# A hybrid decoder block on one core: the first pair's rows picked in turned form, and a new order of the last steps

## The reference, cut to what matters

```python
x = x + hybrid_mixer(rms_norm(x, mix_norm_g), ...)         # mixers, gates, output projection
t = rms_norm(x, ffn_norm_g)                                # 512 tokens
group, expert logits = t @ w_router_group, t @ w_router_expert
# one group of 4 per token, the top 2 of its 8 experts, weights combine (T, 32)
for e in range(32):
    hid = silu(t @ w_expert_gate[e]) * (t @ w_expert_up[e])  # 1024 -> 256
    out += combine[:, e:e+1] * (hid @ w_expert_down[e])      # 256 -> 1024
return rms_norm(x + out, final_norm_g)
```

## Time and profile before

| | us |
|---|---|
| median of 3 runs | 722.11 (720.05 to 722.59) |
| the profiled execution | 720.5 |
| its span, first to last instruction | 718.4 |
| PE busy | 698.4, 97% of the span |
| weight loads (PEld) busy | 514.5, 72% |
| VectorE, ScalarE, GpSimd busy | 371.8, 256.4, 80.1 |
| chain that ended last, share of PE | 90% |
| moved by DMA | 163.52 MB, mean 228 GB/s |

### The profile page before, as it was taken

How to read it: one execution, slowest core, us unless ns; L and a number is a source line. 1 busy time by engine, 2 the same in 40 slices (tenths; PEclk the granted TensorE clock), 3 DMA queues, 4 the chain that set the end, 5 groups by cost and what they waited for, 6 DMA issues and landing times.

```text
span 718.4 us, 10092 instructions
## 1 busy us (share of the span) xinstructions
PE 698.4 (97%) x3967; PEld 514.5 (72%) x3967; DVE 371.8 (52%) x727; ACT 256.4 (36%) x426; POOL 80.1 (11%) x116
## 2 busy tenths in 40 slices
PE   7999999999999999999999999999999999999894
PEld 6888987877877777788888888665555556555442
DVE  6378996357676778755536303751514121212227
ACT  7332134467676776644225212121101111111113
POOL 2001922000010101000003000011211212121000
PEclk9999999999999999999999999999999999999998
DMA  7523244220212222295214598699999999999993
GB/s 240 174 66 111 65 121 147 74 73 16 68 66 73 74 74 74 82 381 181 91 56 183 219 416 303 266 368 365 408 418 419 401 421 421 418 420 417 419 375 141
DMA packets 60208, 163.52 MB, mean 228 GB/s; under 512 B 7846, under 2 KB 39667, under 8 KB 47868
## 3 DMA queue, kind: packets, MB, share of 16 engines
q1 hardware_dynamic: 54668, 150.71, 55.3%
q0 software_dynamic: 5488, 12.11, 4.5%
HBM read 154.64 MB, written 15.99 MB: 238 GB/s over the span
## 4 chain that ended last, share of the span: by engine, by line
PE 90%; DMA 4%; DVE 3%; ACT 1%; issue 1%; SPq 0%; POOLq 0%; DVEq 0%; ACTq 0%
PE psum L1719 31%; PE psum L2146 15%; PE psum L1820 12%; PE psum L2172 8%; PE psum L1999 6%; PE psum L1832 3%; PE psum L2112 2%; DMA ring_e<-y_dram 2%; DVE ring_e L1087 2%; PE psum L1845 1%; PE psum L1875 1%; DMA y_dram<-ye,slots 1%; PE psum L2155 1%; PE psum L1958 1%; PE psum L1910 1%; PE psum L1898 1%
## 5 line engine op out<-in xcount | busy, mean ns | idle before, releaser
L1719 PE MATMUL psum<-xh,wh 128*128 128x512 f32 x256 | 99.9, 390 | 0.8 <-DVE xl L1087 0.8
L1719 PE MATMUL psum<-xh,wl 128*128 128x512 f32 x256 | 99.6, 389 | 0.0
L1719 PE MATMUL psum<-xl,wh 128*128 128x512 f32 x256 | 99.6, 389 | 0.0
L1090 DVE TENSOR_TENSOR wl<-raw,wh 128x1280 fp32r<-128x1280 f32 (+4 forms) x37 | 71.8, 1945 | 24.7 <-ACT wh L780 9.0
L1087 DVE SCALAR_TENSOR_TENSOR hid<-psum,rslot,act_g 128x256 f32<-128x256 f32 x17 | 8.2, 483 | 93.4 <-PE psum L2146 92.8
L1719 PEld LDWEIGHTS psum<-xh,wh 128*128 128x128 f32 x256 | 48.1, 188 | 11.1 <-DVE xl L1087 1.0
L1719 PEld LDWEIGHTS psum<-xh,wl 128*128 128x128 f32 x256 | 48.0, 188 | 9.9
L1719 PEld LDWEIGHTS psum<-xl,wh 128*128 128x128 f32 x256 | 48.1, 188 | 9.8
L1820 PE MATMUL psum<-xh,wh 128*128 128x512 f32 x128 | 51.7, 404 | 0.0
L1820 PE MATMUL psum<-xh,wl 128*128 128x512 f32 x128 | 50.1, 391 | 0.0
L1820 PE MATMUL psum<-xl,wh 128*128 128x512 f32 x128 | 49.9, 390 | 0.0
(11 more groups left out here) (386 smaller groups left out, 1539.6 us busy)
## 6 DMA issues: line engine op xcount, KB each, us to landing
raw<-in_w_gate SPq DMA_DIRECT2D x16, 1024.0 KB, 6.4
raw<-in_w_in SPq DMA_DIRECT2D x9, 1024.0 KB, 5.5
ring_w<-in_w_expert_gate SPq DMA_DIRECT2D x8, 1024.0 KB, 19.8
ring_w<-in_w_expert_up SPq DMA_DIRECT2D x8, 1024.0 KB, 22.4
ring_h<-in_w_expert_down SPq DMA_DIRECT2D x8, 1024.0 KB, 16.5
ring_h<-in_w_expert_gate SPq DMA_DIRECT2D x6, 1024.0 KB, 18.2
ring_e<-in_w_expert_down SPq DMA_DIRECT2D x6, 1024.0 KB, 23.1
ring_e<-in_w_expert_gate SPq DMA_DIRECT2D x6, 1024.0 KB, 21.4
```

What stands on the lines that cost most here:

```text
L1090: return dve.tensor_tensor(dst, src, hi.bitcast(F32), ALU.subtract)
L1719: last = nc.tensor.matmul(dst, a, b, start=start and n == 0, stop=stop and n == len(seq) - 1)
```

## The change

It has three parts. (1) In `choose_rows`, `x2` becomes the stationary operand, 128 features of it at a time (with a step of 8), and `chosen` the moving one. The result comes out turned, in the banks where the transposes would have put it, so the two copies to `xg` and the first turn's transposes go, with the waits for them. (2) In the last turn, `hid` is computed ahead of tile 1's weighted sum. (3) Tile 0's final scaling leaves VectorE: the reciprocal is computed ahead of the adds, ScalarE copies the sum with the scale, and GpSimd multiplies by the gain; SyncE stores tile 0 first, on a semaphore of its own. What else changes are counts at semaphores, and a memset that now covers both halves of `xg`.

```diff
@@ choose_rows (PE)
-                return nc.tensor.matmul(bank[b][:, :], chosen[:, t, :], x2[:, t, b * T:(b + 1) * T], start=t == 0, stop=t == NT - 1)
+                for k in range(4 * b, 4 * b + 4):
+                    last = nc.tensor.matmul(bank[b][:, (k % 4) * P:(k % 4 + 1) * P], x2[:, t, :].rearrange("p (n c) -> p c n", c=KC)[:, k, :],
+                                            chosen[:, t, :], start=t == 0 and k % 4 == 0, stop=t == NT - 1, skip_group_check=True)
+                return last
...
-                choose_rows(NT - 1, b).then_inc(S["routed_ps"], 1)
+                choose_rows(NT - 1, b).then_inc(S["xt_ps"], 1)
@@ x_transposes, expert_pass (PE)
-                if isinstance(c, int) and i == 0:
-                    pe.wait_ge(S["moved_a"], 2 * NT + 1)
-                    pe.wait_ge(S["hot_ready"], ALL_HITS + 1)
-                elif b == 0:
+                if b == 0:
...
-                for b in range(2):
-                    x_transposes(c, 0, first % 2, b)
+                if not isinstance(c, int):
+                    for b in range(2):
+                        x_transposes(c, 0, first % 2, b)
@@ ahead of the expert pass (ScalarE, VectorE, GpSimd)
-            act.wait_ge(S["routed_ps"], NT + 1)
-            act.activation(xg[:, 0, 0:T], bank[0][:, :], ACT.Copy).then_inc(S["moved_a"], 1)
...
-            dve.wait_ge(S["routed_ps"], NT + 2)
-            dve.tensor_copy(xg[:, 0, T:2 * T], bank[1][:, :]).then_inc(S["hot_ready"], 1)
...
-            st.link(pool.memset(xg[:, 1, :], 0.0))
+            st.link(pool.memset(xg[:, :, :], 0.0))
@@ last turn (VectorE)
-                        gather_results(1, EARLY_ROWS)
                     dve.wait_ge(S["silu"], E + 1)
                     dve.wait_ge(S["gu_done"], E + 1)
                     stt(hid[:, :], bank[3][:, 0:FE], rslot[:, column(c, i)], act_g[:, :], ALU.mult, ALU.mult).then_inc(S["hid_r"], 1)
+                    if isinstance(c, int) and i == LAST:
+                        gather_results(1, EARLY_ROWS)
@@ the end (VectorE)
+            dve.wait_ge(S["root"], NT + 2 + NORMED.index(0))
+            dve.reciprocal(stat[:, 2, 0:1], stat[:, 1, 0:1]).then_inc(S["comb"], 1)
             added(2)
-            first_scaled(0)
             added(3)
             first_scaled(2)
@@ the end (ScalarE)
                     final_norm(n, t, TOTALS[t], 3 * NT)
+                    if t == 0:
+                        act.wait_ge(S["comb"], 3)
+                        act.activation(halves(yt[0][:, 1, :]), TOTALS[0], ACT.Copy, scale=stat[:, 2, 0:1]).then_inc(S["norm_step"], 1)
@@ the end (GpSimd)
+            pool.wait_ge(S["tab_in"], 48)
+            pool.wait_ge(S["norm_step"], 2)
+            pool.tensor_tensor(halves(yt[0][:, 1, :]), halves(yt[0][:, 1, :]), halves(gfin), ALU.mult).then_inc(S["norm_step"], 1)
@@ the end (SyncE)
+            sp_e.wait_ge(S["norm_step"], 3)
+            sp_e.dma_start(out_v[0], yt[0][:, 1, :]).then_inc(S["out_done"], 16)
             store_results(0)
```

More of the change, by code:

```diff
@@ L308, in hybrid_trunk @@
             "hi_part xg_ps xg_neg xg_min xg_ln xg_max xg_exp xb_ps xg_free gate_ps br_ps gate_free gate_mul h_add h_hi h_split out_ps x2_ready "
-            "wo_in wo_hi wo_split g_in tab_in x2_out xt2_ps moved_a lg_ps sq2_sum wr_ready slots_in flag_ready lg_act lg_in m_ready routed_ps "
+            "wo_in wo_hi wo_split g_in tab_in x2_out xt2_ps moved_a lg_ps norm_step wr_ready slots_in flag_ready lg_act lg_in m_ready routed_ps "
             "hot_ready slot_ps idx_ready over_ready rs_in rs_ps rs_ready rank_ready turns gf0 gf1 w_ps pick_ready y_hi y_lo y_zero xt_ps xe g_done gu_done silu hid_r "
@@ L606, in store_results @@
                 for n, t in enumerate(NORMED):
-                    sp_e.wait_ge(S["fin_last"], base + n + 1)
+                    if base == 0 and t == 0:
+                        continue
+                    sp_e.wait_ge(S["fin_last"], base + n + (1 if base else 0))
                     sp_e.dma_start(out_v[t], yt[t][:, 1, :]).then_inc(S["out_done"], 16)
+            sp_e.wait_ge(S["norm_step"], 3)
+            sp_e.dma_start(out_v[0], yt[0][:, 1, :]).then_inc(S["out_done"], 16)
             store_results(0)
@@ L623, in _ @@
                 load_results(range(NT))
-                store_results(NT)
+                store_results(NT - 1)
                 sp_e.wait_ge(S["out_done"], 2 * (16 * NT))
@@ L1009, in _ @@
                 token_squares(n)
-            act.wait_ge(S["sq2_sum"], 1)
+            act.wait_ge(S["norm_step"], 1)
             act.activation(stat[:, 1, :], stat[:, 0, :], ACT.Sqrt, bias=eps[:, 0:1], scale=1.0 / D).then_inc(S["root"], 1)
-            act.wait_ge(S["routed_ps"], NT + 1)
-            act.activation(xg[:, 0, 0:T], bank[0][:, :], ACT.Copy).then_inc(S["moved_a"], 1)
             act.wait_ge(S["lg_in"], 1)
@@ L1067, in _ @@
                     final_norm(n, t, TOTALS[t], 3 * NT)
+                    if t == 0:
+                        act.wait_ge(S["comb"], 3)
+                        act.activation(halves(yt[0][:, 1, :]), TOTALS[0], ACT.Copy, scale=stat[:, 2, 0:1]).then_inc(S["norm_step"], 1)
                 else:
-                    act.wait_ge(S["comb"], 2 + t - ADDED + 1)
+                    act.wait_ge(S["comb"], 3 + t - ADDED + 1)
                     final_norm(n, t, halves(yt[t][:, 0, :]), 3 * NT)
@@ L1077, in _ @@
                 for n, t in enumerate(NORMED):
-                    act.wait_ge(S["fin_last"], NT + n)
+                    act.wait_ge(S["fin_last"], NT - 1 + n)
                     final_norm(n, t, TOTALS[t], 4 * NT)
@@ L1422, in _ @@
             dve.wait_ge(S["sq_done"], 3 * NT)
-            dve.reduce_sum(stat[:, 0, :], sq_part[:, :, :], AX.X).then_inc(S["sq2_sum"], 1)
+            dve.reduce_sum(stat[:, 0, :], sq_part[:, :, :], AX.X).then_inc(S["norm_step"], 1)
             for part in range(2):
@@ L1671, in _ @@
             with dve.If(most[0] > SLOT):
-                dve.wait_ge(S["comb"], 2 + NT - ADDED)
+                dve.wait_ge(S["comb"], 3 + NT - ADDED)
                 for t in range(NT):
@@ L2064, in table_products @@
                 if i == SPILL and k == 0:
-                    pe.wait_ge(S["hot_ready"], ALL_HITS + 2)
+                    pe.wait_ge(S["hot_ready"], ALL_HITS + 1)
                     slot_products()
@@ L2188, in _ @@
                 with pe.Fori(1, PASSES) as c:
-                    pe.wait_ge(S["hot_ready"], c + (ALL_HITS + 2))
+                    pe.wait_ge(S["hot_ready"], c + (ALL_HITS + 1))
                     slot_products()
```

## The result

The changed kernel took 728.5 us (median of 4 runs, 727.22 to 731.11), the kernel before beside it 721.3 (4 runs, 720.05 to 722.59): a ratio of 1.0099, with a 95% interval of 1.0065 to 1.0133. The forecast of 720.0 and its range of 717.0 to 723.0 are missed: the change costs about 7 us. The profiled execution of the change took 727.43, with a span of 725.1.

A forecast was written before the change was run, and what follows sets the result against it. PE, busy for 97% of the span, was taken to bound the kernel. 1.5 us at the handover to the experts plus 0.65 at the end made 2.15 off the median of 722.11: 720.0, range 717.0 to 723.0.

The forecast's parts named there:

- The pace of the picks: Turned picks on PE: 0.115 us a record, from router products, so 16 records cost 1.84, as four old ones did.
- the upper end: Picks at 0.145 us a record, from the strided transposes: 64 records cost 1.9 more, run 721.9; chance 0.10.
- loads and products take turns: Picks on PE: loads not overlapped, 0.30 us a record, 11.8 more, run 731.8; loses above about 0.15 a record; chance 0.05.
- The gain of the picks: Handover from routing to experts: first expert product at 470.15 in place of 471.69, 1.5 us earlier.
- That the stream moves with it: Expert pass: weight reloads of 475 to 503, issued as PE frees slots, move 1.5 us earlier too; all 1.5 taken.
- The rival in which the stream stays: Expert pass: DMAs do not move, the 1.5 becomes longer waits for weights, 0.65 is left, run 721.5; chance 0.17.
- The clock is no part of any case: PE's clock: granted at 1.00, the level of 2.4 GHz, in both stretches read, so no cost was assigned.
- Gated product first: Last turn: gated product ahead of tile 1's weighted adds, worth 0.5 us, not 1.1, since `down` weights land at 695.0.
- Tile 0 by ScalarE and GpSimd: Final scalings: VectorE loses one scaling of 1.28 us, GpSimd's product takes 2.5, last scaling ends at 713.25 against 713.90.
- The rival of 3.8: Final scalings: GpSimd's product takes 3.8 us, the end is 0.6 worse than before, run 721.2; chance 0.13.
- the mere stretch of 0.3: Tile 2's scaling beside GpSimd: loses some 0.3 us without waiting fully, end 713.1; the full wait, 713.25, was taken.
- Both edits together: End of the kernel: gated product first and tile 0's moved scaling together save 0.65 us.

The follow-up runs named there:

- picks only: Against the kernel before: turned picks with neighbouring features and the first pair's weights reordered to match, last turn and final scalings as before; 718.68 us, ratio 0.9964.
- The step series: The changed kernel with steps of 2, mostly 3, or 4 elements in the picks' stationary operand in place of 8; 719.61, 723.93 and 729.39 us.
- the quick form: The changed kernel with neighbouring features per pick, and the first pair's gate and up weights and gain read in matching order; 719.28 us, ratio 0.9957 to the kernel before.
- 128 records: The changed kernel with each turned pick split into two products of 64 slot columns, step of 8 kept; 742.67 us.

## Why the prediction was wrong

VectorE's row for the gated product stands once in each turn, so it serves as a clock of the pass. Starts in the profiled executions, in us, and the end of the last scaling:

| turn | before | picks only | the change, neighbouring features | the change |
|---|---|---|---|---|
| 0 | 482.04 | 480.63 | 480.69 | 488.39 |
| 1 | 498.15 | 496.73 | 496.80 | 507.34 |
| 2 | 510.38 | 508.96 | 509.03 | 519.58 |
| 14 | 660.73 | 659.32 | 659.37 | 669.90 |
| 15 | 675.43 | 672.82 | 672.82 | 682.89 |
| 16 | 692.68 | 690.05 | 689.08 | 699.16 |
| end | 713.90 | 711.27 | 710.58 | 720.67 |

The last two columns differ in the step alone, and the first pick's load starts at 459.0 in both. The loss reads off in three pieces: 7.70 at turn 0, which is the picks with the first fall of the clock in them; 2.84 more in turn 1, where the clock was at 0.50 for some 6.8 us; and 0.45 given back, mostly in turn 15, where PE waits less for weights. 7.70 + 2.84 - 0.45 = 10.09, the difference at the end.

**The pace of the picks: the step that failed.** The prediction said "I take 0.115" a record, with 0.145 as the upper end. Measured were 0.24, and 0.26 for the last 16, most of which ran at the lower clock. 64 x (0.24 - 0.115) = 8.0, against 7.70 seen at turn 0. The router row that the 0.115 came from was right about size, type and count, but its stationary operand is contiguous; the transposes had the step but are another kind of instruction. No row of the trace before joins both, so the two ends enclosed nothing, and the range was too narrow. With neighbouring features the record took 0.111 to 0.128, near the forecast.

The Trainium skill (SBUF — State Buffer, Specifications (TRN2)) states that SBUF has lines of 16 bytes, that full bandwidth needs at least two hits in a line, and that crossing to a new one costs. The step series agrees with it: 196 ns with two f32 of a line, 261 in between, 329 and 335 with one. The prediction did not bring that rule in, though the step of 8 stands in the diff; by it the picks would have been a rival with a price of their own. That page also says elsewhere (Door 1: The DMA port swizzle (why `[64,N]` ≈ `[32,N]`)) that steps of up to 4 are free for f32; here 4 is nearly as dear as 8, so the measurement decides for the rule of two hits.

**The rival "loads and products take turns"** named the side, the place and the break-even of 0.15 a record, but not the mechanism. Loads overlap here: 64 of 334 ns fill only 15.6 us. By taking turns the contiguous loads of 192 ns would not fit a record each 0.111. The rule of the Trainium skill that stood beside it, that a load overlaps products only in another row group (TensorE: Matmul & The Clock Gate, Part 3, The mechanism), is not borne out by these full-height records. It had 0.05 of the chances, for want of a mechanism that the trace supported.

**The gain of the picks** was right where the load is quick: first expert product 3.03 after `chosen` where 3.0 was forecast, and 1.41 to 1.46 of the forecast 1.5 kept through turn 14. **That the stream moves with it** held as well: the distance to before stays at 1.41 from turn 0 to turn 14, and then grows by 1.2 in turn 15, where PE's wait for `up` weights was 1.1 (1.3 before), and a wait of 0.7 before the `gate` products, whose cause the trace does not name, is gone. The rival in which the stream stays is refuted for 1.5 us, and for a delay too: 9.19 late at turn 1 is still 9.17 at turn 14. Only turn 15 gives back, 1.71 (the 0.98 of turn 16 is the gated product's own place ahead of tile 1's sums).

**The clock.** "The clock is no part of any case" was wrong. All four runs of the change lie at a mean granted clock of 0.988 to 0.990, the twelve of the quick form at 0.994 to 0.997, those of before beside them spread from 0.987 to 0.997, the ones up to 0.989 at 724.6 to 725.1. In all three kernels with 64 or more loads of 0.33 us (the change, 128 records, step of 4) the clock fell during the picks; in those with quick loads it did not. So the slow picks go with the fall there, in one profile each. The fall in turn 1 came without them too, at the same price: with the old picks and parts 2 and 3, turn 1's gated product started 18.96 after turn 0's (483.93 to 502.89), in the change 18.95, in the kernel before 16.11. Whether the slow picks make that fall likelier is open: it wasn't tried. So 2.84 of the 6.93 between the two profiled times are shown to be the clock's, but not to be the change's.

**Gated product first** was 0.5 in the sum and 0.34 to 0.46 in the runs, with `down` products waiting for the DMA as forecast. **Tile 0 by ScalarE and GpSimd**: GpSimd's product took 2.38 where 2.5 was taken from three smaller ones, and the end 18.06 where 18.25 was. The rival of 3.8 is refuted. Tile 2's scaling, begun at 716.05, ended at 717.89. A full wait until GpSimd's end at 716.81 and 1.28 behind it would give 718.09, the mere stretch of 0.3 717.63; it lies between the two, and the profile's spans on GpSimd are rough, so the rows don't tell a full wait from a stretch. The Trainium skill states a full wait for two SBUF inputs beside a GpSimd read (SBUF — State Buffer, Who interferes with whom); by it the end would be the 718.09, 0.20 later than measured. Both edits together were forecast at 0.65 and measured about 0.7, but the nearness is luck: part 2 brought less than its 0.5, part 3, which had the other 0.15, brought 0.32 to 0.34.

**The sum, corrected**, against before: the forecast -1.5 at the front is +6.35 at turn 0 (64 slow records less what goes); the clock adds 2.84 in turn 1; the waits for weights give back 1.73 up to turn 15, which starts the last turn 7.47 late (695.37 against 687.90); parts 2 and 3 take off 0.70. That leaves 6.77 at the end of the last scaling, against 6.93 between the two profiled times.

## What to carry to other kernels

When a product is turned round, the operand that becomes stationary brings its access pattern with it: look at its step before pricing the load, and take the price from a row with that step and that kind of instruction, not from two rows with one of them each. If no row has both, the range must reach to what the step could cost. Here the step could be moved away, at no cost that the runs show, into the order in which the next weights are read.

## What the runs showed of the hardware

- A plain f32 load of 128x128 took 192 ns contiguous, 196 at a step of 2, 261 at 3, 329 at 4, 335 at 8 elements, and records follow at 0.111 to 0.128 contiguous, 0.17 at 3 (8 in 1.33), 0.22 to 0.26 at 4 and 8. A transpose's load with a step of 8 took 188. Why the transpose is spared is open.
- The step-8 loads lasted as long at a granted clock of 0.50 as at 1.00 (336 ns against 335 as the median, 338 the most of 64; with 128 records 335 at both), while with the step of 4, in the stretch at 0.50 behind the picks, the slot table's contiguous loads lasted 328 in place of 191. In these rows the lower clock costs a strided load nothing, and a contiguous one as much as the step does.
- A product of 128x1024 f32 on GpSimd took 2.38 to 2.39 us, and a VectorE scaling of that size begun beside it 1.84 to 1.85 in place of 1.28, in each of the profiles that had them.
